# A hybrid decoder block on one core: the row scale goes through DRAM, the first weight half to VectorE, the norm weights to GpSimd's queue

## The chip, the cores and the metric

One core of one Trainium2 chip. The metric is device time in microseconds; the kernel is one launch, all weights are read from HBM within it. Lower is better.

## What is computed

One decoder layer on 512 tokens of width 1024, in float32: a sandwich-normed hybrid mixer and a sandwich-normed squared-ReLU MLP. The part the change touches is the beginning: the first norm, and the first columns of the input projection.

```python
def rms_norm(x, g):
    y = x * lax.rsqrt(jnp.mean(x * x, axis=-1, keepdims=True) + EPS)
    return y * g

h = rms_norm(x, norm_mix_pre)            # x: 512 tokens x 1024
z = h @ w_in                             # 1024 x 10240, ten parts
a_h, a_b, a_c, c_a, c_g, s_u, s_v, g_a, g_c, g_s = split(z)
y_a = a_b * causal_dwconv(a_c * a_h, conv_a_w)                 # 3 taps
y_c = silu(layer_norm(causal_dwconv(c_a * sigmoid(c_g), conf_dw_w) + conf_dw_b))
y_s = spatial_gating(gelu(s_u), gelu(s_v), ...)
merged = sigmoid(g_a) * (y_a @ w_branch[0]) + sigmoid(g_c) * (y_c @ w_branch[1]) \
       + sigmoid(g_s) * (y_s @ w_branch[2])
x = x + rms_norm(merged @ w_out, norm_mix_post)
x = x + rms_norm(square(relu(rms_norm(x, norm_ffn_pre) @ w_ff1)) @ w_ff2, norm_ffn_post)
```

## The kernel before, in words

**Products.** Every float32 matrix is split into a high part (rounded to float32r) and a low part (what is left), and a product is three matmuls: high by high, high by low, low by high (lines 1590, 1592, 1594, in `products`). The weights come in *units* of 128x1024, numbered from 0. For each unit SyncE's queue loads `raw` (two slots), ScalarE copies it to `w_hi` (line 683, `split_hi`), VectorE subtracts to `w_lo` (line 1066, `split_lo`), and TensorE runs 24 matmuls of 512 columns. `w_hi` and `w_lo` are rings of four units. The load of a unit waits for `w_lo_ready` of the unit two before it; ScalarE's copy into the ring waits for `unit_done` of the unit four before it.

**The first eight units** (`U_V` 0 to 7) are the columns `s_v`, by token. They don't use the normed x: TensorE multiplies `x * gain` (`c_hi`, `c_lo`), and the scale of each row (1 / rms, `rstd`) is applied behind, as a per-partition scale in the gelu (line 764). x comes transposed as `xt`, eight pieces of 128x512 in five loads (`X_LOADS`); ScalarE makes `c_hi` (line 724, `gain_hi`) and VectorE `c_lo` (line 1089). Unit 0 is loaded and split in two halves, so that TensorE can begin sooner: `half_loaded`, `half_hi`, `half_lo` are the semaphores of its first half, `unit_0` (line 1670) the products. Before it TensorE runs ten matmuls on constants (`keep_warm`, line 1660), which only need GpSimd's four memsets.

**The units from 8 on** (`U_MIX`) are by channel and need x with gain and row scale: `a_hi` and `a_lo`. For that the row scale has to lie along the free dimension of every partition, as `row_rstd` (128x512, in the place of `y_s`). The way there: ScalarE squares and sums the four chunks of x (line 711) behind units 0 and 1, into PSUM banks 4 to 7 as a dump; GpSimd makes `rstd` (lines 582 and 586); TensorE multiplies `rstd`, broadcast, by the identity between two blocks of unit 3 (`spread`, line 1695: four matmuls in the code, eight in the trace) into PSUM bank 7; ScalarE copies that to `row_rstd` (line 757), before its `w_hi` of unit 6. Then VectorE scales `xt` (line 1120, `xn_ready`), ScalarE copies to `a_hi` (line 683), VectorE subtracts to `a_lo` (line 1066). `NORMED_BEHIND` says behind which unit's split this is done for which pieces: here 0 to 3 behind unit 3, 4 to 7 behind unit 4. `glu` in rows of this stretch is `xt`, which lies in its place.

TensorE waits for all eight `act_lo_ready` before unit 8, the first matmul on `a_hi`. Each engine's order is written out by hand; the waits are on semaphores:

```python
for n in range(2 * CH):                    # ScalarE, units 0 to 7
    after(u)
    ...                                    # sums of squares behind units 0 and 1
    if n == CH - 2:
        act.wait_ge(rstd_spread, 1)
        nc.scalar.activation(row_rstd[:, :], ps[:, 2 * CH - 1, :], ACT.Copy)
    split_hi(u.plus(RING))
    xn_hi(NORMED_BEHIND.get(n, ()))
    if n % CH == CH - 1:                   # n = 3 and 7: gelu of four chunks
```

GpSimd's queue holds, in this order: the memsets, the identity, four times `rstd`, the loads of the spatial weights of tiles 0 and 1 (lines 594 and 595), then it waits for VectorE's statistics at about 58 us.

Of the kernel before, what the change touches and what calls it, by code (L numbers as in the profile page):

```python
# [25 lines left out]
F32 = mybir.dt.float32  # L26
F32R = mybir.dt.float32r
ALU = mybir.AluOpType
ACT = mybir.ActivationFunctionType

P = 128
# [3 lines left out]
CH = SEQ // P  # L35
HALF = D // 2
# [11 lines left out]
WARM = 10  # L48
X_LOADS = ((0,), (1,), (2, 3), (4, 5), (6, 7))
SUMSQ_BEFORE = {0: (0, 1), 1: (2, 3)}  # L50
NORMED_BEHIND = {3: (0, 1, 2, 3), 4: (4, 5, 6, 7)}


COL_A = 0
# [11 lines left out]
U_V = 0  # L66
# [170 lines left out]

def build(nc, x_d, xt_d, gain_d, units_d, cols_d, rows_d, ws_d, bs_d, out_d):
    kept_d = nc.dram_tensor("mixed_kept", (SEQ, D), F32, kind="Internal").ap()
    with ExitStack() as ctx:  # L240
        place = {}

# [8 lines left out]
        def sem(name):  # L251
            return ctx.enter_context(nc.semaphore(name))


        raw = sb("raw", [P, RAW, D])
        w_hi = sb("w_hi", [P, RING, D], F32R)
# [8 lines left out]
        c_hi = sb("c_hi", [P, KT, SEQ], F32R)  # L265
# [92 lines left out]
        half_lo = sem("half_lo")  # L358
        gained_hi = sem("gained_hi")
        gained_lo = sem("gained_lo")  # L360
        rstd_spread = sem("rstd_spread")
        row_rstd_ready = sem("row_rstd_ready")
        xn_ready = sem("xn_ready")
        rows_again = sem("rows_again")
# [199 lines left out]
        def _(pool):  # L564
            nc.gpsimd.memset(power[:, :], -0.5).then_inc(consts_ready, 1)
            nc.gpsimd.memset(ident[:, :], 0.0).then_inc(consts_ready, 1)
            nc.gpsimd.memset(mean_of[:, :], 1.0 / D).then_inc(consts_ready, 1)
            nc.gpsimd.memset(ones[:, :].bitcast(F32), 1.0).then_inc(consts_ready, 1)
            pool.wait_ge(consts_ready, 4)
            nc.gpsimd.affine_select(out=ident[:, :], in_=ident[:, :], compare_op=ALU.not_equal,  # L570
                                    fill=1.0, base=0, pattern=[[-1, P]],
# [16 lines left out]

            for c in range(CH):
                inverse_rms(c, c)  # L590

            def load_spatial(j, slot):

                pool.dma_start(ws_raw[:, slot, :], ws_d[j]).then_inc(spatial_loaded[slot], 16)
                pool.dma_start(bs_row[:, slot, :],
                               bs_d[j:j + 1, :].to_broadcast([P, P])).then_inc(spatial_loaded[slot], 16)
# [7 lines left out]

            for j in range(2):
                load_spatial(j, j)

            pool.wait_ge(bn_ready, 3 * CH)
            nc.gpsimd.tensor_scalar(v_rstd[:, 0, :], mv[:, :, 1], 1.0, EPS, ALU.mult,
# [71 lines left out]
        def _(act):  # L681
            def copy_hi(dst, src, scale=1.0):
                return nc.scalar.activation(dst, src, ACT.Copy, scale=scale)  # L683
# [28 lines left out]
                                     accum_out=sumsq[:, n:n + 1]).then_inc(sumsq_ready, 1)  # L712

            act.dma_start(xt[:, 0, :], xt_d[0]).then_inc(xt_loaded[0], 16)
            act.dma_start(gain[:, :], gain_d).then_inc(gain_loaded, 16)
            act.dma_start(xt[:, 1, :], xt_d[1]).then_inc(xt_loaded[1], 16)
            act.wait_ge(consts_ready, 1)
            nc.scalar.activation(sumsq[:, 0:CH], power[:, :], ACT.Copy).then_inc(table_ready, 1)
# [5 lines left out]
                    nc.scalar.activation(c_hi[:, k, :], xt[:, k, :], ACT.Copy,  # L724
                                         scale=gain[:, k:k + 1]).then_inc(gained_hi, 1)

            act.wait_ge(half_loaded, 16)
            copy_hi(w_hi[:, 0, 0:HALF], raw[:, 0, 0:HALF]).then_inc(half_hi, 1)
            act.wait_ge(gain_loaded, 16)
            gain_hi(0)  # L730
            act.wait_ge(raw_loaded[0], 16)
# [12 lines left out]
            for n in range(2 * CH):  # L744
                u = Count(U_V + n)
                after(u)
                for c in SUMSQ_BEFORE.get(n, ()):
                    act.wait_ge(x_loaded[c], 16)
                    if c == 0:
                        act.wait_ge(table_ready, 1)  # L750
                    if c >= 2:
                        act.wait_ge(sumsq_ready, c - 1)
                    sum_squares(c, resid[:, c, :].rearrange("p (b n) -> p b n", b=2),
                                ps[:, CH + 2 * (c % 2):CH + 2 * (c % 2) + 2, :])
                if n == CH - 2:
                    act.wait_ge(rstd_spread, 1)
                    nc.scalar.activation(row_rstd[:, :], ps[:, 2 * CH - 1, :], ACT.Copy).then_inc(row_rstd_ready, 1)
                split_hi(u.plus(RING))
                xn_hi(NORMED_BEHIND.get(n, ()))
                if n % CH == CH - 1:  # L760
                    half = n // CH
                    for c in range(CH):
                        act.wait_ge(rstd_ready, c + 1)
                        nc.scalar.activation(by_token[:, c, half * HALF:(half + 1) * HALF],
                                             ps[:, half * CH + c, :], ACT.Gelu_apprx_tanh,
                                             scale=rstd[:, c:c + 1]).then_inc(v_ready, 1)
# [296 lines left out]
        def _(dve):  # L1063
# [21 lines left out]
            def gain_lo(n):  # L1085

                for k in X_LOADS[n]:
# [2 lines left out]
                                                   in1=c_hi[:, k, :], op0=ALU.mult,  # L1090
                                                   op1=ALU.subtract).then_inc(gained_lo, 1)

            dve.wait_ge(half_hi, 1)
            lo(w_lo[:, 0, 0:HALF], raw[:, 0, 0:HALF], w_hi[:, 0, 0:HALF]).then_inc(half_lo, 1)
            dve.wait_ge(gain_loaded, 16)
# [17 lines left out]
            for n in range(2 * CH):  # L1113
                u = Count(U_V + n)
                after(u)
                split_lo(u.plus(RING))
                ks = NORMED_BEHIND.get(n, ())
                for k in ks:
                    dve.wait_ge(row_rstd_ready, 1)
                    nc.vector.scalar_tensor_tensor(out=xt[:, k, :], in0=xt[:, k, :], scalar=gain[:, k:k + 1],  # L1120
                                                   in1=row_rstd[:, :], op0=ALU.mult,
                                                   op1=ALU.mult).then_inc(xn_ready, 1)
                for k in ks:
                    dve.wait_ge(act_hi_ready, k + 1)
                    lo(a_lo[:, k, :], xt[:, k, :], a_hi[:, k, :]).then_inc(act_lo_ready, 1)
                if n == CH + 1:
                    statistics(0)
# [459 lines left out]
        def _(pe):  # L1587
# [29 lines left out]
                                  k == 0, k == KT - 1)  # L1617
                return mm

            def token_unit(u, piece, half, hi, low, before_block={}):  # L1620
                ready(u)
                for c in range(CH):
                    if c in before_block:
                        before_block[c]()
                    mm = token_block(c, piece, hi, low, w_hi[:, u.ring, :], w_lo[:, u.ring, :],
                                     half * CH + c)
                mm.then_inc(unit_done, 1)
# [59 lines left out]
                mm = unit_0(c_lo, w_hi, k)  # L1687
            mm.then_inc(unit_done, 1)

            def spread():  # L1690

                pe.wait_ge(consts_ready, 5)
                pe.wait_ge(rstd_ready, CH)
                for c in range(CH):
                    mm = nc.tensor.matmul(ps[:, 2 * CH - 1, c * P:(c + 1) * P], rstd[:, c:c + 1].to_broadcast([P, P]),
                                          ident[:, :], start=True, stop=True)
                mm.then_inc(rstd_spread, 1)

            for n in range(1, CH):
                pe.wait_ge(gained_lo, 2 * n + 2)  # L1700
                token_unit(Count(U_V + n), n, 0, c_hi, c_lo, {2: spread} if n == CH - 1 else {})
            for n in range(CH, 2 * CH):
                token_unit(Count(U_V + n), n % CH, n // CH, c_hi, c_lo,
                           {CH - 1: lambda: pe.wait_ge(row_rstd_ready, 1)} if n == CH else {})
            pe.wait_ge(act_lo_ready, KT)

            with pe.Fori(0, KT // 2) as i:
# [186 lines left out]
```

## Time and profile before

| | us |
|---|---|
| median of 3 runs | 961.3 (961.15 to 962.46) |
| the profiled execution: its own time | 959.98 |
| its span, first to last instruction | 958.2 |
| TensorE matmul busy | 948.2 (99%) |
| VectorE, ScalarE, GpSimd busy | 731.4 (76%), 430.6 (45%), 104.4 (11%) |
| mean granted TensorE clock | 0.997 |

The profile's times are of one execution, in microseconds from its first instruction. A row of the timeline gives the start, the duration (for several instructions the stretch they cover), the engine, the line of kernel.py, the operation and its tiles. ACTq, SPq are DMA issues in a queue.

### The profile page before, as it was taken

The numbers are of one execution on the slowest core, as the hardware profiler recorded it, in microseconds if no ns is written. First come the engines' busy times: TensorE is split into PE (matmuls) and PEld (weight loads), VectorE is DVE, ScalarE is ACT, GpSimd is POOL, SyncE is SP. The second block draws the span as 40 slices with busy tenths as digits, with TensorE's granted clock in tenths as the row PEclk, the third lists the DMA queues.
The fourth block names the chain that finished last, engine by engine and source line by source line (L and its number), as shares of the span: only waits on it lengthen the run. The fifth ranks groups of instructions, "written<-read, shape, count | busy, mean of one in ns | idle before, by whom it ended". The sixth has DMA issues, their size and how long they took to land.

```text
span 958.2 us, 13425 instructions
## 1 busy us (share of the span) xinstructions
PE 948.2 (99%) x4838; PEld 809.0 (84%) x4838; DVE 731.4 (76%) x854; ACT 430.6 (45%) x534; POOL 104.4 (11%) x128
## 2 busy tenths in 40 slices
PE   9999999999999999999999999999999999999997
PEld 7888888888888888888888888899889889979985
DVE  4679888888888988886584434599976886796698
ACT  7632333333333322224274323467745745754674
POOL 1100001001100011113100000131101102011110
PEclk9999999999999999999999999999999999999998
DMA  8333223322222122223225333477989679678864
GB/s 325 110 111 105 99 93 96 108 93 93 93 95 102 66 100 96 89 89 132 88 93 215 109 109 110 176 198 192 269 265 245 162 212 246 172 185 260 246 188 132
DMA packets 40731, 142.84 MB, mean 149 GB/s; under 512 B 4720, under 2 KB 4848, under 8 KB 40688
## 3 DMA queue, kind: packets, MB, share of 16 engines
q1 hardware_dynamic: 31728, 111.32, 32.7%
q0 software_dynamic: 7712, 27.27, 15.4%
q10 hardware_dynamic: 1248, 3.67, 1.1%
q8 instruction: 27, 0.44, 0.2%
q14 instruction: 16, 0.13, 0.0%
HBM read 138.05 MB, written 4.19 MB: 148 GB/s over the span
## 4 chain that ended last, share of the span: by engine, by line
PE 82%; DMA 7%; DVE 6%; ACT 3%; issue 2%; SPq 0%; POOL 0%; DVEq 0%; ACTq 0%
PE ps L1590 25%; PE ps L1592 24%; PE ps L1594 24%; DMA glu<-units_in 5%; DVE w_lo L1066 3%; PE ps L1775 2%; PE ps L1779 2%; PE ps L1777 2%; DMA raw_d<-units_in 1%; ACT w_hi L683 1%; PE ps L1716 1%; DVE h_lo L1066 1%; PE ps L1670 1%; ACT h L960 1%; DVE h L1408 1%
## 5 line engine op out<-in xcount | busy, mean ns | idle before, releaser
L1590 PE MATMUL ps<-a_hi,w_hi 128*128 128x512 f32 x576 | 225.7, 392 | 0.0
L1066 DVE TENSOR_TENSOR w_lo<-raw,w_hi 128x1024 fp32r<-128x1024 f32 (+1 forms) x125 | 153.3, 1229 | 94.1 <-ACT w_hi L683 93.4
L1592 PE MATMUL ps<-a_lo,w_hi 128*128 128x512 f32 x576 | 224.2, 389 | 0.0
L1594 PE MATMUL ps<-a_hi,w_lo 128*128 128x512 f32 x576 | 224.1, 389 | 0.0
L683 ACT ACTIVATE w_hi<-raw 128x1024 fp32r<-128x1024 f32 (+1 forms) x125 | 130.2, 1048 | 186.1 <-PE ps L1594 112.9
L1149 DVE SCALAR_TENSOR_TENSOR conf<-glu,cols,conf (+1 forms) x240 | 186.8, 778 | 27.5 <-DVE conf L1149 26.4
L1590 PEld LDWEIGHTS ps<-a_hi,w_hi 128*128 128x128 f32 x576 | 108.1, 188 | 22.7 <-issue 0.5
L1592 PEld LDWEIGHTS ps<-a_lo,w_hi 128*128 128x128 f32 x576 | 108.1, 188 | 22.6 <-issue 0.5
L1594 PEld LDWEIGHTS ps<-a_hi,w_lo 128*128 128x128 f32 x576 | 108.2, 188 | 22.5
L1066 DVE TENSOR_TENSOR w_lo<-glu,w_hi 128x1024 fp32r<-128x1024 f32 x56 | 67.7, 1221 | 37.0 <-ACT w_hi L683 36.9
L1590 PE MATMUL ps<-w_hi,h_hi 128*128 128x512 f32 x224 | 87.9, 393 | 0.4
L1594 PE MATMUL ps<-w_hi,h_lo 128*128 128x512 f32 x224 | 87.3, 390 | 0.0
L1592 PE MATMUL ps<-w_lo,h_hi 128*128 128x512 f32 x224 | 87.3, 390 | 0.0
L683 ACT ACTIVATE w_hi<-glu 128x1024 fp32r<-128x1024 f32 x56 | 58.1, 1053 | 49.4 <-PE ps L1594 20.0
L1775 PE MATMUL ps<-x_plain_hi,w_hi 128*128 128x256 f32 x256 | 73.3, 286 | 0.9 <-DVE h L1399 0.4
L1777 PE MATMUL ps<-x_plain_lo,w_hi 128*128 128x256 f32 x256 | 72.4, 283 | 0.0
L1779 PE MATMUL ps<-x_plain_hi,w_lo 128*128 128x256 f32 x256 | 72.4, 283 | 0.0
L1775 PE MATMUL ps<-x_diff_hi,w_hi 128*128 128x256 f32 x192 | 54.5, 284 | 0.0
L1777 PE MATMUL ps<-x_diff_lo,w_hi 128*128 128x256 f32 x192 | 54.3, 283 | 0.0
L1779 PE MATMUL ps<-x_diff_hi,w_lo 128*128 128x256 f32 x192 | 54.3, 283 | 0.0
L1590 PEld LDWEIGHTS ps<-w_hi,h_hi 128*128 128x128 f32 x224 | 42.1, 188 | 12.0 <-DVE w_lo L1066 3.0
L1775 PEld LDWEIGHTS ps<-x_plain_hi,w_hi 128*128 128x128 f32 x256 | 49.0, 192 | 2.4 <-DVE h L1399 1.3
(177 smaller groups left out, 1608.7 us busy)
## 6 DMA issues: line engine op xcount, KB each, us to landing
raw<-units_in SPq DMA_DIRECT2D x141, 512.0 KB, 3.2
glu<-units_in SPq DMA_DIRECT2D x26, 512.0 KB, 6.5
glu<-units_in POOLq DMA_DIRECT2D x26, 512.0 KB, 8.3
raw_d<-units_in POOLq DMA_DIRECT2D x24, 512.0 KB, 6.5
raw_v<-units_in SPq DMA_DIRECT2D x16, 512.0 KB, 5.9
raw_d<-units_in SPq DMA_DIRECT2D x8, 512.0 KB, 6.2
conf<-x_in SPq DMA_DIRECT2D x4, 512.0 KB, 6.0
conf<-x_in ACTq DMA_DIRECT2D x1, 2048.0 KB, 8.0
```

Source lines behind the costliest of these rows:

```text
L683: return nc.scalar.activation(dst, src, ACT.Copy, scale=scale)
L960: nc.scalar.activation(h, h, ACT.Relu, scale=sign).then_inc(rectified, 1)
L1066: return nc.vector.tensor_tensor(dst, src, hi, ALU.subtract)
L1149: nc.vector.scalar_tensor_tensor(out=conf[:, tile, :], in0=glu[:, tile, k:k + SEQ], scalar=cols[:, tile, COL_CONF + k:COL_CONF + k + 1], i ...
L1408: nc.vector.tensor_tensor(h_of[first if n == 1 else second][:, :, :], h_of[first][:, :, :], h_of[second][:, :, :], ALU.subtract).then_inc( ...
L1590: nc.tensor.matmul(ps[:, bank, :], left_hi, right_hi, start=first, stop=False, skip_group_check=on_top)
L1592: nc.tensor.matmul(ps[:, bank, :], left_hi, right_lo, start=False, stop=False, skip_group_check=on_top)
L1594: return nc.tensor.matmul(ps[:, bank, :], left_lo, right_hi, start=False, stop=final, skip_group_check=on_top)
L1670: mm = nc.tensor.matmul(ps[:, c, :], left[:, k, c * P:(c + 1) * P], right[:, 0, w], start=start, stop=False)
L1775: nc.tensor.matmul(out, w_hi[:, u % RING, w], hi[:, k, :], start=not free and k == 0, stop=False, skip_group_check=free)
L1777: nc.tensor.matmul(out, w_hi[:, u % RING, w], low[:, k, :], start=False, stop=False, skip_group_check=free)
L1779: mm = nc.tensor.matmul(out, w_lo[:, u % RING, w], hi[:, k, :], start=False, stop=k == CH - 1, skip_group_check=free)
```

## The change

Three edits. The load of the norm weights `gain` (128x8) leaves ScalarE's queue, where it stood between the two first pieces of `xt`, for GpSimd's, behind the four memsets. The high part of unit 0's first half is made by VectorE with a `tensor_copy`, in front of the low part, where ScalarE had made it. And `row_rstd` is no longer spread by TensorE and copied by ScalarE: GpSimd stores the 128x4 `rstd` to a DRAM tensor of 512 numbers, issues the loads of the spatial weights, waits for the store, and loads the 512 numbers into every partition. Scaling and splitting x stand one unit later. TensorE's waits change: for the sums of squares before unit 4, whose banks they dump in, in place of the wait for `row_rstd` before the last block of unit 4.

```diff
-NORMED_BEHIND = {3: (0, 1, 2, 3), 4: (4, 5, 6, 7)}
+NORMED_BEHIND = {4: (0, 1, 2, 3), 5: (4, 5, 6, 7)}
...
+    rstd_d = nc.dram_tensor("row_rstd", (CH, P), F32, kind="Internal").ap()
...
             nc.gpsimd.memset(ones[:, :].bitcast(F32), 1.0).then_inc(consts_ready, 1)
+            pool.dma_start(gain[:, :], gain_d).then_inc(gain_loaded, 16)
             pool.wait_ge(consts_ready, 4)
...
             for c in range(CH):
                 inverse_rms(c, c)
+            pool.wait_ge(rstd_ready, CH)
+            pool.dma_start(rstd_d.rearrange("c p -> p c"), rstd[:, 0:CH],
+                           allow_slow_non_contiguous=True).then_inc(rstd_stored, 16)
...
             for j in range(2):
                 load_spatial(j, j)
+            pool.wait_ge(rstd_stored, 16)
+            pool.dma_start(row_rstd[:, :].rearrange("p (c t) -> p c t", c=CH),
+                           rstd_d.unsqueeze(0).to_broadcast([P, CH, P])).then_inc(row_rstd_ready, 16)
...
             act.dma_start(xt[:, 0, :], xt_d[0]).then_inc(xt_loaded[0], 16)
-            act.dma_start(gain[:, :], gain_d).then_inc(gain_loaded, 16)
             act.dma_start(xt[:, 1, :], xt_d[1]).then_inc(xt_loaded[1], 16)
...
-            act.wait_ge(half_loaded, 16)
-            copy_hi(w_hi[:, 0, 0:HALF], raw[:, 0, 0:HALF]).then_inc(half_hi, 1)
             act.wait_ge(gain_loaded, 16)
             gain_hi(0)
...
-                if n == CH - 2:
-                    act.wait_ge(rstd_spread, 1)
-                    nc.scalar.activation(row_rstd[:, :], ps[:, 2 * CH - 1, :], ACT.Copy).then_inc(row_rstd_ready, 1)
...
+            dve.wait_ge(half_loaded, 16)
+            nc.vector.tensor_copy(w_hi[:, 0, 0:HALF], raw[:, 0, 0:HALF]).then_inc(half_hi, 1)
             dve.wait_ge(half_hi, 1)
...
-                    dve.wait_ge(row_rstd_ready, 1)
+                    dve.wait_ge(row_rstd_ready, 16)
...
-            def spread():
-
-                pe.wait_ge(consts_ready, 5)
-                pe.wait_ge(rstd_ready, CH)
-                for c in range(CH):
-                    mm = nc.tensor.matmul(ps[:, 2 * CH - 1, c * P:(c + 1) * P], rstd[:, c:c + 1].to_broadcast([P, P]),
-                                          ident[:, :], start=True, stop=True)
-                mm.then_inc(rstd_spread, 1)
...
-                token_unit(Count(U_V + n), n, 0, c_hi, c_lo, {2: spread} if n == CH - 1 else {})
+                token_unit(Count(U_V + n), n, 0, c_hi, c_lo)
+            pe.wait_ge(sumsq_ready, CH)
             for n in range(CH, 2 * CH):
-                token_unit(Count(U_V + n), n % CH, n // CH, c_hi, c_lo,
-                           {CH - 1: lambda: pe.wait_ge(row_rstd_ready, 1)} if n == CH else {})
+                token_unit(Count(U_V + n), n % CH, n // CH, c_hi, c_lo)
+            pe.wait_ge(consts_ready, 5)
             pe.wait_ge(act_lo_ready, KT)
```

How the instructions stand. First ScalarE from the last sums of squares to its gelu, before (`y_s` is `row_rstd`, `glu` is `xt`, `wide` the gelu's result):

```order
L711 ACTIVATE ps,sumsq<-conf 128x1024 [waits sumsq_ready,x_loaded3]
L683 ACTIVATE w_hi<-raw 128x1024 [waits unit_done,raw_loaded1]
L757 ACTIVATE y_s<-ps 128x512 [waits rstd_spread,unit_done]
L683 ACTIVATE w_hi<-raw 128x1024 [waits unit_done,raw_loaded0]
L683 ACTIVATE w_hi<-raw 128x1024 [waits unit_done,raw_loaded1]
L683 ACTIVATE a_hi<-glu 128x512 [waits xn_ready] x4
L764 ACT_TABLE_LOAD
L764 ACTIVATE wide<-ps,rstd 128x512 [waits rstd_ready] x4
L683 ACTIVATE w_hi<-raw 128x1024 [waits unit_done,raw_loaded0]
L683 ACTIVATE a_hi<-glu 128x512 [waits xn_ready] x4
```

And with the change, the same stretch:

```order
L719 ACTIVATE ps,sumsq<-conf 128x1024 [waits sumsq_ready,x_loaded3]
L691 ACTIVATE w_hi<-raw 128x1024 [waits unit_done,raw_loaded1]
L691 ACTIVATE w_hi<-raw 128x1024 [waits unit_done,raw_loaded0]
L691 ACTIVATE w_hi<-raw 128x1024 [waits unit_done,raw_loaded1]
L766 ACT_TABLE_LOAD
L766 ACTIVATE wide<-ps,rstd 128x512 [waits rstd_ready] x4
L691 ACTIVATE w_hi<-raw 128x1024 [waits unit_done,raw_loaded0]
L691 ACTIVATE a_hi<-glu 128x512 [waits xn_ready] x4
L691 ACTIVATE w_hi<-raw 128x1024 [waits unit_done,raw_loaded1]
L691 ACTIVATE a_hi<-glu 128x512 [waits xn_ready] x4
```

The copy from PSUM is gone, and the table load, the gelu and the high part of unit 8 now stand before both groups of `a_hi`.

GpSimd with the change, from the last `rstd` on (`y_s<-row_rstd` is the load into every partition); before, the first and the last of these DMA rows were not there:

```order
L588 TENSOR_TENSOR rstd<-meansq,power 128x1 [waits meansq_step]
L594 DMA row_rstd<-rstd 128x4x1 [waits rstd_ready]
L599 DMA ws_raw<-ws_in 128x128
L600 DMA bs_row<-bs_in 128x128
L599 DMA ws_raw<-ws_in 128x128
L600 DMA bs_row<-bs_in 128x128
L613 DMA y_s<-row_rstd 128x512 [waits rstd_stored]
L617 TENSOR_SCALAR v_rstd<-mv 128x4 [waits bn_ready]
```

Six DMAs stand here where there were four, and the statistics' row waits behind the load.

## Rows read from the trace of the kernel before

**Rows 1.** The page's busy times, its first line
```profile
PE 948.2 (99%) x4838; PEld 809.0 (84%) x4838; DVE 731.4 (76%) x854; ACT 430.6 (45%) x534; POOL 104.4 (11%) x128
```

**Rows 2.** Waits of TensorE, whole span: us in total, times, longest
```profile
PE ps L1660 <- POOL ones L568: 1.4, 1, 1.4
PE ps L1775 <- DVE h L1399: 0.4, 1, 0.4
...
PE ps L1670 <- ACT c_hi L724: 0.2, 1, 0.2
```

**Rows 3.** Timeline, 0 to 8 us: start, us, engine, line, operation
```profile
0.81 0.42 ACTq L714 DMA_DIRECT2D glu<-xt_in  x1
...
1.12 0.20 POOL L568 MEMSET ones<- 128x128 f32 x1
...
1.26 0.45 ACTq L715 DMA_DIRECT2D gain<-gain_in  x1
...
1.38 4.63 PE L1660 MATMUL ps<-ones 128*128 128x512 f32 x10 [1.38 <-POOL ones L568]
...
4.41 0.63 ACT L683 ACTIVATE w_hi<-raw 128x512 fp32r<-128x512 f32 x1 [0.69 <-DMA raw<-units_in]
5.07 0.69 DVE L1066 TENSOR_TENSOR w_lo<-raw,w_hi 128x512 fp32r<-128x512 f32 x1 [5.07 <-ACT w_hi L683]
5.48 0.72 ACT L724 ACTIVATE c_hi<-glu,gain 128x512 fp32r<-128x512 f32 x1 [0.44 <-DMA gain<-gain_in]
...
6.25 1.78 PE L1670 MATMUL ps<-w_hi,c_hi 128*128 128x512 f32 x4 [0.24 <-ACT c_hi L724]
...
7.88 1.09 PE L1670 MATMUL ps<-w_lo,c_hi 128*128 128x512 f32 x4
```

**Rows 4.** DMA issues in short stretches: count, KB, us from issue to landing
```profile
glu<-xt_in ACTq DMA_DIRECT2D x1, 256.0 KB, 3.8
...
gain<-gain_in ACTq DMA_DIRECT2D x1, 4.0 KB, 4.2
...
bs_row<-bs_in POOLq DMA_DIRECT2D x1, 64.0 KB, 4.8
...
ws_raw<-ws_in POOLq DMA_DIRECT2D x1, 64.0 KB, 2.0
```

**Rows 5.** VectorE by line and form, whole span: busy, mean ns
```profile
L1137 DVE TENSOR_SCALAR wide<-wide,mv,v_rstd 128x1024 f32<-128x1024 f32 x4 | 3.0, 807 | 1.4 <-POOL v_rstd L612 1.4
```

**Rows 6.** Timeline of TensorE around the spread, 25.8 to 27.2 us
```profile
25.82 0.39 PE L1594 MATMUL ps<-w_hi,c_lo 128*128 128x512 f32 x1
26.05 1.05 PE L1695 MATMUL ps<-ident,rstd 128*128 128x128 f32 x8
...
27.17 0.39 PE L1592 MATMUL ps<-w_lo,c_hi 128*128 128x512 f32 x1
```

**Rows 7.** Timeline of GpSimd, last `rstd` and first load behind it
```profile
23.61 0.56 POOL L586 TENSOR_TENSOR rstd<-meansq,power 128x1 f32<-128x1 f32 x1
24.12 0.78 POOL L594 DMA_DIRECT2D ws_raw<-ws_in  x1
```

**Rows 8.** Timeline of ScalarE, 30 to 40 us
```profile
30.73 1.06 ACT L683 ACTIVATE w_hi<-raw 128x1024 fp32r<-128x1024 f32 x1 [1.99 <-DMA raw<-units_in]
...
36.45 1.28 ACT L764 ACT_TABLE_LOAD   x1
37.74 2.42 ACT L764 ACTIVATE wide<-ps,rstd 128x512 f32<-128x512 f32 x4
```

**Rows 9.** Timeline of VectorE, 31 to 38 us
```profile
31.89 1.23 DVE L1066 TENSOR_TENSOR w_lo<-raw,w_hi 128x1024 fp32r<-128x1024 f32 x1 [1.82 <-ACT w_hi L683]
33.03 2.73 DVE L1120 SCALAR_TENSOR_TENSOR glu<-glu,gain,y_s 128x512 f32<-128x512 f32 x4
35.68 2.49 DVE L1066 TENSOR_TENSOR a_lo<-glu,a_hi 128x512 fp32r<-128x512 f32 x4
```

**Rows 10.** Timeline of TensorE, the first matmul on the normed x
```profile
51.46 0.39 PE L1590 MATMUL ps<-a_hi,w_hi 128*128 128x512 f32 x1
```

More of the change, by code:

```diff
@@ L360, in build @@
         gained_lo = sem("gained_lo")
-        rstd_spread = sem("rstd_spread")
+        rstd_stored = sem("rstd_stored")
         row_rstd_ready = sem("row_rstd_ready")
@@ L1618, in token_block, with token_unit @@
                 return mm
-            def token_unit(u, piece, half, hi, low, before_block={}):
+            def token_unit(u, piece, half, hi, low):
                 ready(u)
                 for c in range(CH):
-                    if c in before_block:
-                        before_block[c]()
                     mm = token_block(c, piece, hi, low, w_hi[:, u.ring, :], w_lo[:, u.ring, :],
```

## The prediction

> **What bounds the kernel now.** First the page's busy times: TensorE is busy for 948.2 of 958.2 us, every other engine for at most 76% [rows 1]. So only what TensorE executes, or waits for, can move the time. Then its waits: over the whole span it waited 1.4 us for GpSimd's constants at the start, 0.24 us for `c_hi` before unit 0, and 0.4 us near the end [rows 2]; the rest of the idle time is behind its last matmul. The whole kernel is one chain of matmuls with two things in the beginning that this change can reach: the gap before unit 0, and the spread of the row scale. Everything else that it moves is on ScalarE, VectorE, GpSimd and the queues, and costs nothing as long as TensorE still finds its inputs there.
>
> The timeline shows the gap: ten matmuls on constants fill 1.38 to 6.01, and the first real one starts at 6.25 [rows 3]. It waits for `c_hi`, which ScalarE makes from 5.48 to 6.20, and that waits for the norm weights: issued at 1.26, they land 4.2 us later, at 5.46, while the first piece of x, issued at 0.81, lands at 4.61 and the first weight half has been copied by 5.04 [rows 3, 4]. So the norm weights, 4 KB, are last.
>
> **Edit 1 and 2, the start.** GpSimd's memsets end at 1.12 + 0.20 = 1.32; the issue of `gain` stands there. What a load from that queue takes is shown by the spatial loads, 64 KB: 2.0 us at the least and 4.8 at the most [rows 4]. So `gain` lands between 3.3 and 6.1. I take the middle, 3.5 us, and 4.8: the 16 DMA engines are loaded here, but `gain` is small and no longer stands behind 256 KB of x in its own queue. `c_hi` then needs 0.72, from 4.8 to about 5.55. It could not start before 4.61 anyhow.
>
> VectorE copies the weight half from about 4.4. Nothing in the trace is a plain copy of this form. From above, the subtraction of the same half takes 0.69; from below, `TENSOR_SCALAR` needs 0.81 for 1024 elements, so about 0.4 for 512 [rows 3, 5]. Ready at 4.8 to 5.1, against 5.04 by ScalarE: no matter, `c_hi` at 5.55 is later. The low part follows at 5.5 to 5.8. TensorE first needs it at its fifth matmul, after 7 us. So the copy costs nothing; its cover is `c_hi`, and without it, it would cost at most 0.1.
>
> With `c_hi` at 5.55, TensorE goes from the constants to unit 0 without a gap. The gain is 0.24 at least, and up to 0.44, as a matmul that follows at once starts 0.15 to 0.2 before the end of the last one (6.25 + 1.78 is 8.03, and the next began at 7.88 [rows 3]). But the four products from 6.25 took until 7.88, 0.41 each, where later ones take 0.23 [rows 3, 6]. If that slow stretch ends at the same moment, 0.44 us of earlier start is worth one matmul more before it, 0.44 x 0.23 / 0.41 = 0.25. I take **-0.3**. The bounds: with `gain` at 6.1, `c_hi` ends at 6.84 and the start is 0.64 later than now; with no slow stretch at all behind the start, 0.44 + 4 x (0.41 - 0.23) = 1.1 earlier.
>
> The Trainium skill speaks against both edits. Its page SBUF — State Buffer (section on the two separate sides of SBUF) says that a float32 `tensor_copy` on VectorE shuts GpSimd out of their shared port, so that it can't write the descriptors of its DMAs; by it, `gain` would come later by the copy's length if the two met. In the rows they don't: GpSimd's issues take about 0.8, so this one is over by 2.1, and the copy starts at 4.4 [rows 3, 7]. And DMA: Bandwidth & Descriptors (Latency and other measured facts) gives about 1 us to the first byte from GpSimd's queue and 0.6 from ScalarE's. By that, an estimate from this page and the 4.2 us of before, `gain` would land at 5.9 and the start would be 0.5 later.
>
> **Edit 3, the spread on TensorE.** It goes. The matmul before it starts at 25.82 and the spread at 26.05; behind 25.82 the second next product would start at 26.28 and does at 27.17 [rows 6]. So **-0.89**. This is time of the bounding engine, with no cover. ScalarE's copy of it (0.6) goes too, off the path.
>
> **What takes its place.** The last `rstd` is there at 23.61 + 0.56 = 24.17 [rows 7]. Then GpSimd's queue issues the store and four loads (at most 0.78 each [rows 7]), waits, and issues the load. The store is unlike anything in the trace: 512 numbers of 4 bytes, each alone in DRAM. From below, both transfers take 2.0 as the fastest load does, but GpSimd is free only at 24.17 + 5 x 0.78 = 28.1, so the scale is there at 30.1. From above, the store has 512 pieces where a spatial load has 128: four times 4.8, plus 4.8 for the load, gives 48.2. I take 4.8 for each, nearest to one loaded transfer: the store lands at 29, **the row scale at about 34**. Behind it on GpSimd stands only the work on VectorE's statistics, long after.
>
> Who needs it, and when? VectorE, now one unit later. I follow the new order with durations of before. ScalarE's `w_hi` of unit 7 waits for its load and starts at 30.73, which nothing changes; it ends at 31.8 [rows 8]. Table load and gelu take 1.28 + 2.42, to 35.5. `w_hi` of unit 8 starts there. Before, VectorE's `w_lo` began 1.16 after such a start and the scaling of x 1.14 behind that (30.73, 31.89, 33.03), and from the scaling's start to the end of four `a_lo` it took 35.68 + 2.49 - 33.03 = 5.14 [rows 8, 9]. So the scaling starts at 37.8 and the first four `a_lo` are done at 42.9; another `w_lo` 1.14; the second four at 49.2. TensorE comes to unit 8 at 51.46 less what it has gained, 50.3 [rows 10]. **The margin is 1.1 us**, and the row scale may come up to 3.8 us later than I take it before VectorE waits, 4.9 before TensorE does: the latter point is 38.9. Cost taken: 0. That is the thinnest cover of the change: before, by the same rows, the normed x was ready some four us ahead.
>
> TensorE's new wait, for the sums of squares before unit 4, is met: the last `rstd` is made from them by 24.17, and unit 4 starts ten matmuls of 0.23 behind the 27.17 [rows 6], less 0.9, near 28.6. What stands in the queues at the start moves by less than 0.5: the second piece of x is issued one issue of 0.45 earlier [rows 3], and behind unit 0 TensorE waited for nothing until near the end [rows 2].
>
> **Sum.** -0.3 - 0.9 + 0 = -1.2 us on the profiled execution's 959.98, 958.8. That execution lies 1.3 below the median of the runs, 961.3; taken from the median the forecast is **960.1**. It is 0.12%, and about 0.2% (1.9 us) is what a measurement of this kernel can tell from no change.
>
> **The rivals.**
>
> *The norm weights come late* (14%). For: loads from GpSimd's queue took up to 4.8, and the DMA engines are busiest here. Against: the load is small and has a queue for itself. With `gain` at 6.1 the start loses 0.64, the spread still gives 0.89: 961.3 - 0.25 = 961.0. Another way to it is an issue that is still at work at 4.4, in spite of the rows, and is held up there by VectorE's copy: at most 0.69 on top of 4.8 gives 5.5, the start of before, and 960.4. This is the rule of the Trainium skill's page SBUF — State Buffer; the other page's puts `gain` at 5.9, between the two.
>
> *The row scale comes late, and the kernel is slower* (8%). The place is TensorE's wait for `a_lo` before unit 8. From a landing at 38.9 on, each us costs one; from 40.1 the whole gain is eaten; from 42.0 on the kernel is slower by over 0.2%. At the upper bound, 48.2, it stands still for 9.3 us, which gives 961.3 - 1.2 + 9.3 = 969.4; at 44, halfway between the bounds' upper part, 965.2. Against: most of a small transfer's time can't be its bytes, as 4 KB took 4.2 and 256 KB 3.8 [rows 4], and nothing says that the count of pieces weighs fourfold.
>
> *The margin breaks without it* (9%): unit 7's load comes later, pushed by 512 small packets in the same engines, and with it ScalarE's whole order. Two us there are 0.9 of standing still: 961.0.
>
> *The slow stretch ends sooner* (9%): without the gap the matmuls reach 0.23 each from the start of unit 0. Then -1.1 - 0.9 = -2.0: 959.3. For it: there is a gap of 0.24 just before. Against: ten matmuls without a gap were slow as well, 4.63 for ten.
>
> That the change doesn't do what it says can be left out for the spread, whose matmuls are gone in the built order; for the start it is the first rival.
>
> **How the numbers follow.** The forecast has 60%. Faster by over 0.2%: the last rival, and a little of the forecast by scatter, 0.11. Slower: most of the second rival, 0.07. The rest, 0.82, is within 0.2%. The range takes in the fourth and the two middle cases with the scatter of the runs shown (1.3 us), 959.0 to 961.9, and leaves out the late row scale.
>
> **What would show it.** In the new profile: no matmul on `ident`; TensorE's wait before unit 0 gone, or grown if the weights are late; the landing of `gain` against 5.46; unit 8's first matmul at about 50.3 in place of 51.46; the store and the load of the row scale with a sum near 10 us from 24.2; VectorE's scaling of x at about 37.8, waiting for ScalarE and not for a DMA. I am wrong if TensorE shows a wait before unit 8, or if unit 8 comes at 50.3 and the time hasn't followed.

## The result, and the profile after

The changed kernel takes 967.73 us (966.51 to 967.84, 4 runs), the kernel before on the same chip 961.22 (958.69 to 962.46): a ratio of 1.0072, 95% interval 1.0057 to 1.0087. It is 6.5 us slower; the forecast was 1.2 faster, with a range up to 961.9. Here and below a ratio comes from the runs with its own interval; it need not equal the quotient of the two medians beside it.

| | before | after |
|---|---|---|
| span of the profiled execution | 958.2 | 964.8 |
| TensorE matmul busy | 948.2 | 948.5 |
| unit 0 starts | 6.25 | 7.46 |
| unit 1 starts | 12.45 | 13.03 |
| ScalarE's high part of unit 7 starts | 30.73 | 38.10 |
| unit 8 starts | 51.46 | 56.76 |

TensorE is as busy as before; it waits more. Its waits over the whole span in the changed kernel, in the columns of [rows 2]:

```profile
PE ps L1594 <- DVE a_lo L1068: 5.5, 1, 5.5
PE ps L1672 <- ACT c_hi L731: 1.4, 1, 1.4
PE ps L1662 <- POOL ones L569: 1.4, 1, 1.4
PE ps L1769 <- issue: 0.4, 1, 0.4
```

The first one is new: 5.5 us before unit 8, for the last low part of the normed x. The second was 0.24. The timeline of TensorE there shows what each of the two costs:

```profile
1.38 4.64 PE L1662 MATMUL ps<-ones 128*128 128x512 f32 x10 [1.38 <-POOL ones L569]
7.46 1.20 PE L1672 MATMUL ps<-w_hi,c_hi 128*128 128x512 f32 x4 [1.44 <-ACT c_hi L731]
8.49 1.07 PE L1672 MATMUL ps<-w_lo,c_hi 128*128 128x512 f32 x4
...
13.03 0.39 PE L1594 MATMUL ps<-w_hi,c_hi 128*128 128x512 f32 x1
...
50.88 0.39 PE L1598 MATMUL ps<-w_hi,c_lo 128*128 128x512 f32 x1
56.76 0.79 PE L1594 MATMUL ps<-a_hi,w_hi 128*128 128x512 f32 x1 [5.49 <-DVE a_lo L1068]
57.35 0.63 PE L1596 MATMUL ps<-a_lo,w_hi 128*128 128x512 f32 x1
...
60.77 0.51 PE L1594 MATMUL ps<-a_hi,w_hi 128*128 128x512 f32 x1
61.11 0.39 PE L1596 MATMUL ps<-a_lo,w_hi 128*128 128x512 f32 x1
```

Unit 0 starts 1.21 us later, yet unit 1 only 0.58, since its first four products take 1.03 (7.46 to 8.49) where they took 1.63 [rows 3]. Without a wait unit 8 would have started at 50.88 + 0.23 = 51.11, 0.35 before the old 51.46: from +0.58 to -0.35, the missing spread has given 0.93. Then TensorE stands still until 56.76, +5.30 against before. And behind that ten matmuls take 4.35 us (56.76 to 61.11), where ten at 0.227 take 2.27: another 2.08, +7.4 in all. The granted clock of short stretches says why (columns: TensorE, weight loads, VectorE, ScalarE, GpSimd busy; granted clock; DMA share; GB/s):

```profile
51.00:55.00 4.00, 0.27 (x2) 0.00 (x0) 4.00 (x7) 2.84 (x5) 0.00 (x0) 0.90 0.41 131
55.00:57.00 2.00, 0.24 (x1) 0.24 (x2) 2.00 (x5) 2.00 (x3) 0.00 (x0) 0.50 0.02 4
...
60.00:61.00 1.00, 1.00 (x4) 0.81 (x3) 1.00 (x2) 0.00 (x0) 0.00 (x0) 0.50 0.07 16
61.00:62.00 1.00, 1.00 (x5) 0.82 (x5) 1.00 (x4) 0.00 (x0) 0.00 (x0) 1.00 0.77 250
```

The clock fell to 0.50, the 1.2 GHz level, while TensorE stood still, and was back at 1.00 only at 61. At the turn into the MLP, some 560 us on, the distance is still 7.3 (first transpose at 622.1 against 614.8); behind it 0.65 comes back, which is within what that part differs by from profile to profile, as the experiments show.

What was late? The timeline of the other engines, from GpSimd's store to ScalarE's gelu:

```profile
23.58 0.56 POOL L588 TENSOR_TENSOR rstd<-meansq,power 128x1 f32<-128x1 f32 x1
24.45 0.85 POOL L594 DMA_DIRECT2D row_rstd<-rstd  x1 [0.31 <-POOL rstd L588]
...
34.38 0.54 POOL L613 DMA_DIRECT2D y_s<-row_rstd  x1 [6.92 <-DMA row_rstd<-rstd]
...
38.10 1.06 ACT L691 ACTIVATE w_hi<-raw 128x1024 fp32r<-128x1024 f32 x1 [10.52 <-DMA raw<-units_in]
39.17 1.28 ACT L766 ACT_TABLE_LOAD   x1
40.47 2.42 ACT L766 ACTIVATE wide<-ps,rstd 128x512 f32<-128x512 f32 x4
```

The DMA issues of the same stretch, in the columns of [rows 4]:

```profile
row_rstd<-rstd POOLq DMA_DIRECT2D x1, 2.0 KB, 9.6
...
raw<-units_in SPq DMA_DIRECT2D x1, 512.0 KB, 12.1
...
y_s<-row_rstd POOLq DMA_DIRECT2D x1, 256.0 KB, 6.1
```

Two things come late. The store takes 9.6 us and the load 6.1, so the row scale is there at 34.4 + 6.1 = 40.5. And the load of unit 7, issued by SyncE's queue at 25.9 and with nothing to do with the row scale, takes 12.1 us where it took 4.7. ScalarE waits 10.5 us for it, at 38.10 and not 30.73, and everything behind it in ScalarE's order comes 7.4 later: table load, gelu, the high part of unit 8, and with that VectorE's scaling at 45.09. By then the row scale had long landed; the load of unit 7 came last. Over 28 to 34 us the DMA engines moved 16 to 31 GB/s with a busy share above 0.5:

```profile
28.00:30.00 2.00, 2.00 (x10) 1.68 (x9) 0.91 (x1) 0.00 (x0) 0.00 (x0) 1.00 0.56 16
30.00:32.00 2.00, 2.00 (x10) 1.66 (x9) 0.00 (x0) 0.00 (x0) 0.00 (x0) 1.00 0.59 31
32.00:34.00 2.00, 2.00 (x11) 1.65 (x10) 0.00 (x0) 0.00 (x0) 0.00 (x0) 1.00 0.52 20
```

They were occupied and moved next to nothing. Before, they moved 289, 121 and 152 GB/s in these stretches. The time is booked to the load's own packets and not to the store's: from 28 to 34 us SyncE's queue shows 29 packets with 53.2% of the engines' time, about 1.8 us each, and GpSimd's queue 2.4%. Before, SyncE's queue had 282 packets there with 44.7%, about 0.15 us each.

### The profile page after: what moved, and what is told of

Read it like the earlier page. It is cut to its first block, busy times and chain, and to the rows that moved or that the text cites. A ratio compares the mean times of both kernels' runs of the same rounds, so it can differ in the third digit from the quotient of the medians.

```text
span 964.8 us, 13410 instructions
## 1 busy us (share of the span) xinstructions
PE 948.5 (98%) x4830; PEld 809.5 (84%) x4830; DVE 731.7 (76%) x855; ACT 429.8 (45%) x532; POOL 106.3 (11%) x131
## 4 chain that ended last, share of the span: by engine, by line
PE 79%; DMA 9%; DVE 7%; ACT 3%; issue 1%; POOL 0%; SPq 0%; DVEq 0%; ACTq 0%; POOLq 0%
PE ps L1594 24%; PE ps L1598 24%; PE ps L1596 24%; DMA glu<-units_in 5%; DVE w_lo L1068 3%; PE ps L1769 2%; DMA raw<-units_in 2%; PE ps L1771 2%; PE ps L1773 2%; ACT w_hi L691 1%; DMA raw_d<-units_in 1%; PE ps L1710 1%; ACT h L962 1%; DVE glu L1124 1%; DMA gain<-gain_in 1%
## 5 line engine op out<-in xcount | busy, mean ns | idle before, releaser
L1594 PEld LDWEIGHTS ps<-w_hi,h_hi 128*128 128x128 f32 x224 | 42.1, 188 | 11.4 <-DVE w_lo L1068 2.5
```

The costliest lines, as they stand in the source:

```text
L1594: nc.tensor.matmul(ps[:, bank, :], left_hi, right_hi, start=first, stop=False, skip_group_check=on_top)
```

## The experiments

Theory A: the store of single numbers holds up the DMA engines, the load of unit 7 with them, and TensorE pays by standing still and by the clock behind it. The rivals: the late norm weights (B); the wait for the row scale or the later place of the scaling (C).

### One part of the change at a time

**Edit 3 alone** (norm weights and first high part as before):

```diff
-            pool.dma_start(gain[:, :], gain_d).then_inc(gain_loaded, 16)
...
+            act.dma_start(gain[:, :], gain_d).then_inc(gain_loaded, 16)
...
+            act.wait_ge(half_loaded, 16)
+            copy_hi(w_hi[:, 0, 0:HALF], raw[:, 0, 0:HALF]).then_inc(half_hi, 1)
...
-            dve.wait_ge(half_loaded, 16)
-            nc.vector.tensor_copy(w_hi[:, 0, 0:HALF], raw[:, 0, 0:HALF]).then_inc(half_hi, 1)
```

> Only the third edit: the row scale through DRAM, the scaling of x one unit later; the norm weights and the first high part as before. Theory A (the store of 512 single numbers holds up the 16 DMA engines, the load of unit 7 lands near 38 us and TensorE stands still before unit 8, then runs ten matmuls at the lower clock): start at 6.25 as before, -0.9 for the spread, +5.5 to 6.2 standing still, +2.1 behind it: 6.5 to 7.5 us over before. Rival B (the late norm weights are the cause, or half of it): under 3 us over before.

Measured: 968.44 against 959.67, ratio 1.0092 (1.0075 to 1.0108), 8.8 us over. The high part of unit 7 starts at 39.62, TensorE waits 7.9 us. Rival B falls: this edit alone is at least as slow as all three. It is over the range given. The store was issued 1.1 us later than in the changed kernel (25.59), because ScalarE's squares came later, and unit 8 started 1.5 later than there (58.29); the wait is longer still, since unit 1 came 0.9 sooner than there (12.12) and TensorE was at unit 8 that much earlier.

**Edits 1 and 2 alone**, on the kernel before: its `gain` line moved to GpSimd, its `copy_hi` line to VectorE.

> Only edits 1 and 2: norm weights in GpSimd's queue, first high part by VectorE; the spread on TensorE as before. Theory A: the weights land near 6.6, unit 0 starts 1.2 us later, but its matmuls run at 0.23 each from the start, so unit 1 comes 0.6 later: +0.4 to +0.8 us. Rival B: 3 us or more over before.

Measured: 961.82 against 959.67, ratio 1.0028 (1.0015 to 1.0041). In the trace `gain` takes 5.1 us from its issue at 1.43, unit 0 starts at 7.34 and unit 1 at 12.91, +0.46, as expected; unit 8 comes 0.46 late too, with no wait. The time is 2 us over, outside the expected 0.4 to 0.8. The rest is not in the part that the edits touch: from the first transpose to the last matmul this profile has 337.2 us and that of before 335.9. This stretch, the same instructions in all kernels, took between 334.4 and 338.9 us in the fourteen profiles of this study, so a difference of a microsecond can't be traced there. What the rest is stays open; all three edits with the store repaired, which have the same late start, do not show it (at the end of this section).

**The store alone**, added to the kernel before, read by nobody:

```diff
+            pool.wait_ge(rstd_ready, CH)
+            pool.dma_start(rstd_d.rearrange("c p -> p c"), rstd[:, 0:CH],
+                           allow_slow_non_contiguous=True).then_inc(rstd_stored, 16)
...
             for j in range(2):
                 load_spatial(j, j)
+            pool.wait_ge(rstd_stored, 16)
             pool.wait_ge(bn_ready, 3 * CH)
```

> The kernel before, plus only the store of the 512 numbers behind GpSimd's last row scale; nothing reads it. Theory A: the load of unit 7 lands near 38 as in the changed kernel, its w_hi starts near 38.1, and in the order of before the last a_lo comes 7.4 us later, at 54.9, against 51.46: TensorE stands still for 3 to 4 us, plus 1 to 2 us at the lower clock: +3.5 to +6 us. Rival C (it is not the store but the wait for the row scale's load, or the later place of the scaling): no change within 1 us.

Measured: 968.69 against 959.67, ratio 1.009 (1.0073 to 1.0107): 9.0 us for 2 KB that nobody reads; GpSimd's wait for them stands before work that comes only at about 58 us. The timeline of this kernel around unit 7's load and before unit 8:

```profile
25.42 0.99 POOL L594 DMA_DIRECT2D row_rstd<-rstd  x1 [0.31 <-POOL rstd L588]
...
39.43 1.06 ACT L689 ACTIVATE w_hi<-raw 128x1024 fp32r<-128x1024 f32 x1 [10.46 <-DMA raw<-units_in]
...
56.44 0.79 PE L1596 MATMUL ps<-a_hi,w_hi 128*128 128x512 f32 x1 [4.60 <-DVE a_lo L1072]
```

The store took 9.9 us to land. The wait is 4.6, and the granted clock is 0.50 from 56 to 62. Theory A holds; the cost, above its 3.5 to 6, shows at the first transpose: 622.6 against 614.8.

**The later place of the scaling alone** (`NORMED_BEHIND` with 4 and 5, spread on TensorE as before):

> The kernel before, with only the scaling of x one unit later (4 and 5 in place of 3 and 4). Theory A: the margin worked out before holds, unit 8 starts when unit 7 ends: within 0.3 us of before, no wait of TensorE before unit 8. Rival C (the order is the cause): TensorE waits before unit 8 by over 2 us.

Measured: 960.01 against 959.67, ratio 1.0005 (0.9993 to 1.0017), no wait before unit 8. The margin worked out in the prediction was there: the last low part of x ends at 51.23, and unit 8 starts at 52.12. Rival C falls.

### What makes the store slow

**128 pieces of 16 bytes** in place of 512 of 4, in edit 3 alone. The numbers lie by partition in DRAM, so VectorE has to read the row scale with a stride (the load, not shown, takes the 512 numbers as one row):

```diff
-            pool.dma_start(rstd_d.rearrange("c p -> p c"), rstd[:, 0:CH],
-                           allow_slow_non_contiguous=True).then_inc(rstd_stored, 16)
+            pool.dma_start(rstd_d.rearrange("o (p c) -> (o p) c", c=CH), rstd[:, 0:CH]).then_inc(rstd_stored, 16)
...
-                                                   in1=row_rstd[:, :], op0=ALU.mult,
+                                                   in1=row_rstd[:, :].rearrange("p (t c) -> p c t", c=CH),
```

> The third edit alone, with the numbers stored partition by partition: 128 pieces of 16 bytes in place of 512 of 4; VectorE reads the row scale with a stride of four numbers. Theory A1 (the count of pieces sets it): the store lands within 2 to 4 us, unit 7's w_hi starts by 32, TensorE has no wait before unit 8; -0.9 for the spread: 958.8 us, 0.4 to 1.2 us under before. Rival A2 (any small store to DRAM in this place blocks the DMA engines for some 10 us): as with 512 pieces, 7 to 9 us over before.

Measured: 964.77 against 960.31, ratio 1.0037 (1.0024 to 1.005). The mechanism went as expected and the time did not: the store landed after 3.4 us, unit 7's load took 4.8, its high part started at 31.73. (That was forecast from the count of pieces, a reason that two runs below refute.) But TensorE still waited 2.4 us before unit 8, for this:

```profile
31.73 1.06 ACT L688 ACTIVATE w_hi<-raw 128x1024 fp32r<-128x1024 f32 x1 [3.12 <-DMA raw<-units_in]
...
38.72 4.31 DVE L1123 SCALAR_TENSOR_TENSOR glu<-glu,gain,y_s 128x512 f32<-128x512 f32 x4
```

Four scalings with the strided operand take 4.31 us, against 2.73 [rows 9]; twice 1.6 us, on a margin of one. My repair brought its own loss, and the clock added to it. Unit 8 starts at 53.52, +2.06, but the first transpose comes 3.7 later (618.5). The granted clock of short stretches, columns as above:

```profile
53.00:54.00 1.00, 0.48 (x2) 0.44 (x3) 1.00 (x3) 1.00 (x3) 0.00 (x0) 1.00 0.00 0
...
55.00:56.00 1.00, 1.00 (x4) 0.81 (x3) 1.00 (x2) 0.64 (x2) 0.00 (x0) 0.50 0.00 0
...
58.00:59.00 1.00, 1.00 (x6) 0.84 (x5) 1.00 (x3) 0.00 (x0) 0.00 (x0) 1.00 0.85 274
```

It fell about a microsecond after the work had resumed, and was back at 1.00 by 58: some 1.6 us on top of the wait.

**The 512-piece store from ScalarE's queue**, edit 3 alone otherwise:

```diff
-            pool.wait_ge(rstd_ready, CH)
-            pool.dma_start(rstd_d.rearrange("c p -> p c"), rstd[:, 0:CH],
-                           allow_slow_non_contiguous=True).then_inc(rstd_stored, 16)
...
+                if n == CH - 2:
+                    act.wait_ge(rstd_ready, CH)
+                    act.dma_start(rstd_d.rearrange("c p -> p c"), rstd[:, 0:CH],
+                                  allow_slow_non_contiguous=True).then_inc(rstd_stored, 16)
```

> The third edit alone, with the 512-piece store issued from ScalarE's queue, behind its squares, in place of GpSimd's. Theory A1 (pieces in the DMA engines): it lands some 10 us after its issue at 26, unit 7's load is held up until 39 as before the move: 6 to 9 us over before. Rival D (it is GpSimd's making of descriptors, or its queue): lands within 5 us, unit 7's load near 31, at most 1 us from before.

Measured: 968.76 against 960.31, ratio 1.0076 (1.0061 to 1.0091). The store took 9.0 us and unit 7's load 11.4. It is not GpSimd's queue, nor its making of descriptors.

**Half of the numbers**, 256, unread, on the kernel before (`rstd[:, 0:2]`):

> The kernel before plus a store nobody reads, of 256 single numbers, half as many as in the added store measured already (512: landing after 9.9 us, +9.0 us). Theory A1: it lands after 5 to 6 us, unit 7's w_hi starts 5 us sooner, near 34.5, and the last a_lo comes at about 51, at TensorE's door: 0 to 1.5 us over before. Rival A2 (fixed time): as the whole one, +9.

Measured: 966.45 against 960.31, ratio 1.0063 (1.0047 to 1.0079); 9.1 us to land, the high part of unit 7 at 38.82. Neither came true: half the pieces are not half the time, so the count (A1) falls, and 16-byte pieces in the run above had already refuted a fixed time (A2). What is left is the size of a piece, or where the numbers lie.

**512 single numbers 64 bytes apart**, unread, on the kernel before (the lines are against those of the store added above):

```diff
-    rstd_d = nc.dram_tensor("row_rstd", (CH, P), F32, kind="Internal").ap()
+    rstd_d = nc.dram_tensor("row_rstd", (CH, P, 16), F32, kind="Internal").ap()
...
-            pool.dma_start(rstd_d.rearrange("c p -> p c"), rstd[:, 0:CH],
+            pool.dma_start(rstd_d[:, :, 0].rearrange("c p -> p c"), rstd[:, 0:CH],
```

> The kernel before plus the unread store of 512 single numbers, now 64 bytes apart in DRAM. 256 single numbers took 9.1 us to land, 512 took 9.9, and 128 pieces of 16 bytes 3.4, so the count alone does not set it. Theory E (many engines write into the same short stretch of DRAM, one after another): apart they land within 3 to 5 us, unit 7's w_hi starts by 33, at most 1 us over before. Rival F (a piece of 4 bytes is slow wherever it lies): 9 to 10 us to land, +8 to +9 us.

Measured: 960.1 against 960.3, ratio 0.9999 (0.9987 to 1.0011). Its store's issue row, and ScalarE behind the load of unit 7:

```profile
row_rstd<-rstd POOLq DMA_DIRECT2D x1, 2.0 KB, 2.8
```

```profile
30.95 1.06 ACT L689 ACTIVATE w_hi<-raw 128x1024 fp32r<-128x1024 f32 x1 [1.97 <-DMA raw<-units_in]
```

The same engine, queue, count and size of pieces, landing after 2.8 us and not 9.9, and unit 7's load takes 4.2 us and not 12.5. For pieces of 4 bytes this settles it: whether they are neighbours decides.

**128 single numbers side by side**, one column, unread (`rstd[:, 0:1]`):

> The kernel before plus an unread store of one column, 128 single numbers, side by side in 512 bytes. Theory E: the 512 bytes of one row are written one after another, and the four rows beside each other, so it still takes 8 to 9 us and the time is 5 to 8 us over before. Theory A1 (count of pieces, in engines of eight partitions each): 3 to 4 us to land, within 1 us of before.

Measured: 964.4 against 960.3, ratio 1.0039 (1.0021 to 1.0058); 8.0 us for 512 bytes. One row of 128 neighbours takes nearly as long as four. The time is 4.1 over, a little under the expected five to eight. The store was issued sooner here, at 24.50, and the high part of unit 7 came at 37.17. TensorE waited 3.1 us; unit 8 started 2.71 late (54.17), the first transpose 4.4 (619.2), with a granted clock of 0.50 from 56 to 58.

The stores beside each other, which is the whole argument; the first four are read by nobody, the others feed `row_rstd`:

| store | pieces | to land, us | high part of unit 7 at | ratio |
|---|---|---|---|---|
| 4 rows, side by side, added | 512 x 4 B | 9.9 | 39.43 | 1.0090 |
| 2 rows, side by side, added | 256 x 4 B | 9.1 | 38.82 | 1.0063 |
| 1 row, side by side, added | 128 x 4 B | 8.0 | 37.17 | 1.0039 |
| 64 bytes apart, added | 512 x 4 B | 2.8 | 30.95 | 0.9999 |
| as in edit 3, ScalarE's queue | 512 x 4 B | 9.0 | 38.01 | 1.0076 |
| side by side, edit 3 alone | 128 x 16 B | 3.4 | 31.73 | 1.0037 |
| side by side, edit 3 with the copy (below) | 128 x 16 B | 1.9 | 31.58 | 1.0002 |
| side by side, all three edits with the copy (below) | 128 x 16 B | 1.8 | 31.47 | 1.0004 |

The Trainium skill's page DMA: Bandwidth & Descriptors (Specifications) says that below 512 bytes the engines read, modify and write. No trace here shows such a read, and that alone does not tell these stores apart: all pieces here are under 512 bytes, and those 64 bytes apart land in 2.8 us.

So slow are pieces that are both neighbours and of 4 bytes: 128 neighbours of 4 bytes take 8.0 us, 128 neighbours of 16 bytes, four times the data, 1.8 to 3.4. Where between 4 and 16 bytes, or between 4 and 64 bytes of distance, it turns was not measured. Nor is it the number of packets: each of the four added stores is 32 packets in the trace, the fast one too, and the store from ScalarE's queue 528. Those 528 took 1.5% of the engines' time from 24 to 41 us, SyncE's loads beside them 59.1% (32.3% before). So the store is not what fills the engines; the loads' packets are long while it is under way. Where they wait, at one another or at the memory, is not shown.

### What is left of the change without its store

**Edit 3 with 16-byte pieces and one reordering copy on GpSimd**, loaded into a tile that is free then, so that VectorE reads without a stride:

```diff
-            pool.dma_start(row_rstd[:, :].rearrange("p (c t) -> p c t", c=CH),
-                           rstd_d.unsqueeze(0).to_broadcast([P, CH, P])).then_inc(row_rstd_ready, 16)
+            pool.dma_start(u_act[:, :], rstd_d.to_broadcast([P, SEQ])).then_inc(row_rstd_loaded, 16)
+            pool.wait_ge(row_rstd_loaded, 16)
+            nc.gpsimd.tensor_copy(row_rstd[:, :].rearrange("p (c t) -> p c t", c=CH),
+                                  u_act[:, :].rearrange("p (t c) -> p c t", c=CH)).then_inc(row_rstd_ready, 1)
```

> The third edit alone, stored as 128 pieces of 16 bytes, loaded into a free tile, and put in order once by a copy on GpSimd (about 1.5 us, in its idle time), so that VectorE reads the row scale without a stride. Theory (what was left in the run with 16-byte pieces was only VectorE's slower read, 4.31 in place of 2.73 us for four, twice): row scale ready near 36, before VectorE wants it at 38 to 39, no wait of TensorE before unit 8, -0.9 for the spread: 0.4 to 1.2 us under before. Rival (the traffic of the loads moves unit 7's load, or the copy comes late): still 1 us or more over before.

Measured: 960.62 against 960.3, ratio 1.0002 (0.999 to 1.0015). TensorE and the copy:

```profile
33.15 1.78 POOL L614 COPY y_s<-u_act 128x512 f32<-128x512 f32 x1 [4.15 <-DMA u_act<-row_rstd]
...
50.70 0.39 PE L1596 MATMUL ps<-a_hi,w_hi 128*128 128x512 f32 x1
```

Unit 8 starts at 50.70 with no wait, 0.76 before the old 51.46, and the first transpose 0.8 before its old time. So the spread's 0.9 is real, and it is too small for this measurement: the expected 0.4 to 1.2 was not seen in the time, whose interval reaches 1.0 us under before.

**The norm weights first in ScalarE's queue**, high part by VectorE, spread as before:

```diff
+            act.dma_start(gain[:, :], gain_d).then_inc(gain_loaded, 16)
             act.dma_start(xt[:, 0, :], xt_d[0]).then_inc(xt_loaded[0], 16)
-            act.dma_start(gain[:, :], gain_d).then_inc(gain_loaded, 16)
```

> The start alone: the norm weights first in ScalarE's queue, ahead of x, and the first high part by VectorE; the spread on TensorE as before. Theory (the weights' place in a hardware queue decides): they land by 4.4, the first piece of x by 5.0, c_hi at 5.1 to 5.8, no gap before unit 0: 0.1 to 0.5 us under before. Rival (the queue order does not matter, all lands near 5.4): no change.

Measured: 961.51 against 960.31, ratio 1.0005 (0.9996 to 1.0015), no gain. The weights land after 2.8 us, at 3.6, but x, now behind them, comes 4.0 after 1.26, at 5.3. Unit 0 starts at 6.15, 0.1 sooner, and then waits up to 1.1 us for the second piece. Of the two orders tried in this queue neither has both early.

**All three edits with the store repaired**, the reordering copy added to the changed kernel:

> The changed kernel, all three edits, with only its store repaired: 128 pieces of 16 bytes and the copy on GpSimd that puts them in order. Theory: nothing is left of the 5.5 us before unit 8 nor of the lower clock behind it; the spread gives 0.9, the late norm weights cost 0.6 at unit 1: unit 8 near 51 in the trace, and 0 to 2 us over before in the time. Rival G (the margin of the later scaling is too thin once unit 0 starts late): TensorE waits before unit 8 by over 1 us, 2 us or more over before.

Measured: 960.82 against 960.41, ratio 1.0004 (0.9991 to 1.0017). Unit 0 starts at 7.38, unit 1 at 12.97, unit 8 at 51.05 without a wait. With 16-byte pieces and the copy the whole change neither costs nor brings anything that this measurement can tell (the interval reaches from 0.9 us under to 1.6 over). No kernel of this study beats the one before.

## Why the prediction was wrong

**The step that failed** is the sentence on ScalarE's `w_hi` of unit 7, which "waits for its load and starts at 30.73, which nothing changes". It started at 38.10. I priced the store by its landing alone, for those who wait for it, and gave its traffic to no one else; the unread store shows that this traffic alone costs 9.0 us. The rest of that chain held: with 7.4 us put in at unit 7, its 49.2 for the last low part becomes 56.6, and unit 8 started at 56.76. The rival "the margin breaks without it" named this mechanism, 512 small packets pushing unit 7's load, and sized it at 2 us and 0.9 of standing still, with a chance of 9%; it was 7.4 us and 5.5. Its reason, the many packets, was not it: the store is 32 packets in the trace.

**The store's own price** was bounded rightly, 2.0 to 19 us, and taken at 4.8 as nearest to one loaded transfer; it was 9.6, and the row scale came at 40.5 in place of 34. By the prediction's own sums that would have been late for VectorE (37.8) and for TensorE's door (38.9) even with unit 7 on time; no run shows that case. I argued against the upper end that the count of pieces need not weigh fourfold. That was right, the count hardly weighs, and beside the point: that they are neighbours of 4 bytes does, and no row of before could show it.

**The clock** stood in no case of standing still. It cost 2.1 us on top of 5.5. The second rival's rule, each us late costs one, leaves it out, and even the shortest wait here, 2.4 us, cost 1.6 more.

**The spread**, -0.89: right; 0.93 here, and unit 8 came 0.76 sooner in the repaired edit 3.

**The start**, -0.3: wrong sign. `gain` took 5.2 us from an issue at 1.43 (6.66), beyond the upper end of 6.1 that the spatial loads gave, and the start was 1.21 later. The first rival had the mechanism at 14%; of it only 0.58 reached unit 1. That was luck of the profiles: the first four products took 1.63 before and 1.03 after, and 1.01 to 1.31 in the twelve others, whether the start was late or not. A sooner start might have brought little, too: in seven of the ten profiles that keep the start of before TensorE waited 0.37 to 0.52 us for the low part of unit 1. The estimate from the Trainium skill's page DMA: Bandwidth & Descriptors (Latency and other measured facts) was 5.9, nearer to 6.66 than my choice of 4.8, and still short: the landing took 5.2 us against 4.2 from ScalarE's queue, 1.0 more and not 0.4. The copy on VectorE took 0.43, within 0.4 to 0.69, and was over by 4.9 with GpSimd's issue done at 2.2: it cost nothing. The two did not meet, so no run here tests the rule of the Trainium skill's page SBUF — State Buffer (SBUF: two separate sides) on the shared port.

**The margin** of 1.1 us for the later scaling: right. With the order alone moved, and again in both repaired kernels, TensorE did not wait before unit 8; the last low part was done 0.9, 0.8 and 1.2 us ahead.

## What to carry to other kernels

A store is priced twice: by when it lands, and by what it does to every transfer beside it. Numbers of 4 bytes from many partitions, laid side by side in DRAM, are the worst form measured here; give each partition its own 16 bytes and reorder on an idle engine, or space the numbers 64 bytes apart. When a wait of two us or more is put before TensorE, add what its clock takes to come back: 1.6 to 2.8 us in this kernel.

## What the runs showed that was not expected

- 128 neighbouring 4-byte numbers take 8.0 us to land, 512 of them 9.9, 512 of them 64 bytes apart 2.8, 128 neighbouring pieces of 16 bytes 1.8 to 3.4. While such a store is under way a 512 KB load beside it takes 11.1 to 12.5 us and not 4.7, from either kind of queue.
- After 5.5 us without work the granted clock was 0.50, and it stayed there for 4.3 us after the work had resumed. After waits of only 2.4 us (strided reads) and 3.1 us (one row stored) the work resumed at 1.00, the clock fell about a microsecond later, and it cost 1.6 and 1.7 us all the same (the delay at the first transpose less that of unit 8). The loss did not grow with the wait: the seven profiles that wait before unit 8, for 2.4, 3.1, 3.9, 4.6, 5.5, 6.0 and 7.9 us, lost 1.6, 1.7, 1.6, 2.8, 2.0, 1.9 and 1.6 us behind it.
- `SCALAR_TENSOR_TENSOR` with one operand at a stride of four numbers took 1.15 us and not 0.75 (mean of eight).
- The slow matmuls at the start do not end at a fixed place: the ten on constants took 4.64 us in one profile and 3.86 in that of the added store.
